# Whole-chunk weight loads outside the expert loops, with the order of the expert rows and gates changed on GpSimd and VectorE

## What is computed

```python
for l in range(DEPTH):                      # DEPTH = 2, D = 1024
    mod = silu_c @ w_ada[l] + b_ada[l]      # [6 * D]: shifts, scales, gains; the same for the context
    h = rmsnorm(x, norm1_g[l]) * (1.0 + sc1) + sh1
    x = x + g1 * token_mixers(h, ...)       # projections, two attentions, a Fourier mix, gated merge, output
    h = rmsnorm(x, norm2_g[l]) * (1.0 + sc2) + sh2
    x = x + g2 * grouped_moe(h, ...)
return rmsnorm(x_lat, final_norm_g)

def grouped_moe(h, ...):
    scores = sigmoid(h @ router_w)          # 16 experts in 4 groups
    # one group for each token, its best 2 of 4 experts, their scores normalized: gate
    hid = silu(h @ w_g[e]) * (h @ w_u[e]) * gate
    return hid @ w_d[e]                     # summed over the experts e of the token
```

## Time and profile before

| | us |
|---|---|
| median of the runs (3 runs, 1233.89 to 1234.39) | 1234.01 |
| the profiled execution, its own time | 1235.45 |
| its span in the profile | 1233.7 |
| PE busy in it | 1182.4 |
| ACT busy | 610.9 |
| DVE busy | 760.0 |
| POOL busy | 58.9 |

### The profile page before, as it was taken

How to read it: one execution, slowest core, us unless ns; L and a number is a source line. 1 busy time by engine, 2 the same in 40 slices (tenths; PEclk the granted TensorE clock), 3 DMA queues, 4 the chain that set the end, 5 groups by cost and what they waited for, 6 DMA issues and landing times.

```text
span 1233.7 us, 17788 instructions
## 1 busy us (share of the span) xinstructions
PE 1182.4 (96%) x6618; PEld 940.8 (76%) x6618; DVE 760.0 (62%) x1237; ACT 610.9 (50%) x962; POOL 58.9 (5%) x77
## 2 busy tenths in 40 slices
PE   6999999899999999999999998999999989999997
PEld 4677555588888878878888886886599987878886
DVE  4563646524423546757985585847746567568995
ACT  4342555633233334446864474536645445457883
POOL 0010000002000000400000010100000001100000
PEclk8999999999999999999999998999989999999999
DMA  9722499738332005767997697332655505759992
GB/s 363 280 88 65 157 392 341 272 103 168 107 103 88 33 1 184 255 219 219 404 351 220 195 337 265 103 103 69 219 183 183 186 18 203 262 186 332 403 378 96
DMA packets 69588, 250.71 MB, mean 203 GB/s; under 512 B 7968, under 2 KB 9152, under 8 KB 69248
## 3 DMA queue, kind: packets, MB, share of 16 engines
q1 hardware_dynamic: 62864, 225.66, 53.3%
q0 software_dynamic: 6640, 23.92, 5.2%
HBM read 237.45 MB, written 12.10 MB: 202 GB/s over the span
## 4 chain that ended last, share of the span: by engine, by line
PE 84%; DVE 5%; DMA 5%; ACT 3%; issue 2%; POOL 1%; SPq 1%; DVEq 0%; ACTq 0%; PEldq 0%; POOLq 0%
PE bank L1798 22%; PE bank L1799 22%; PE bank L1800 22%; DMA raw<-weights 3%; PE bank L1886 3%; PE bank L2066 3%; PE bank L2109 2%; PE bank L2091 2%; DVE lo L1086 1%; PE bank L2001 1%; DMA hu<-by_slot 1%; ACT w_hi L671 1%; PE bank L2350 1%; DMA by_slot<-xtok,slot_i 1%; PE bank L2380 1%
## 5 line engine op out<-in xcount | busy, mean ns | idle before, releaser
L1086 DVE TENSOR_TENSOR lo<-raw,w_hi 128x1024 fp32r<-128x1024 f32 x328 | 401.7, 1234 | 264.1 <-ACT w_hi L671 262.6
L671 ACT CAST w_hi<-raw 128x1024 fp32r<-128x1024 f32 x328 | 343.2, 1051 | 309.8 <-PE bank L1800 298.2
L1798 PE MATMUL bank<-h_hi,w_hi 128*128 128x512 f32 (+1 forms) x512 | 178.3, 348 | 3.1 <-DVE lo L1086 1.5
L1799 PE MATMUL bank<-h_lo,w_hi 128*128 128x512 f32 (+1 forms) x512 | 176.7, 345 | 0.0
L1800 PE MATMUL bank<-h_hi,lo 128*128 128x512 f32 (+1 forms) x512 | 176.3, 344 | 0.0
L1798 PE MATMUL bank<-w_hi,h_hi 128*128 128x512 f32 (+1 forms) x320 | 127.2, 397 | 2.1 <-DVE h_lo L1550 1.4
L1800 PE MATMUL bank<-w_hi,h_lo 128*128 128x512 f32 (+1 forms) x320 | 123.7, 387 | 0.0
L1799 PE MATMUL bank<-lo,h_hi 128*128 128x512 f32 (+1 forms) x320 | 123.6, 386 | 0.0
L1798 PEld LDWEIGHTS bank<-h_hi,w_hi 128*128 128x128 f32 x512 | 97.9, 191 | 21.1 <-issue 6.3
L1800 PEld LDWEIGHTS bank<-h_hi,lo 128*128 128x128 f32 x512 | 97.9, 191 | 11.6
L1799 PEld LDWEIGHTS bank<-h_lo,w_hi 128*128 128x128 f32 x512 | 98.0, 191 | 11.2
(11 more groups left out here) (312 smaller groups left out, 1891.3 us busy)
## 6 DMA issues: line engine op xcount, KB each, us to landing
raw<-weights SPq DMA_DIRECT2D x424, 512.0 KB, 5.9
y_by_slot<-yring POOLq DMA_DIRECT2D x10, 512.0 KB, 7.9
by_slot<-zeros POOLq DMA_DIRECT2D x5, 512.0 KB, 5.6
x<-tokens SPq DMA_DIRECT2D x4, 512.0 KB, 5.7
nab<-na_bias POOLq DMA_DIRECT2D x2, 1024.0 KB, 8.3
hu<-by_slot POOLq DMA_DIRECT2D x2, 1024.0 KB, 11.9
hu<-by_slot POOLq DMA_DIRECT2D x1, 1536.0 KB, 10.2
rp<-rope POOLq DMA_DIRECT2D x2, 512.0 KB, 4.2
```

What stands on the lines that cost most here:

```text
L671: nc.scalar.copy(w_hi[:, g % N_HI, :], raw[:, ring_slot[c], o:o + HALF]).then_inc(hi_done, 1)
L1086: nc.vector.tensor_tensor(lo[:, ring_slot[c], o:o + HALF], raw[:, ring_slot[c], o:o + HALF], w_hi[:, g % N_HI, :].bitcast(F32), ALU.subtra ...
L1798: nc.tensor.matmul(o, l_hi, r_hi, start=start, stop=False)
L1799: nc.tensor.matmul(o, l_hi, r_lo, start=False, stop=False)
```

## The change

Five things are edited.

1. Outside the expert loops a chunk is one load of 1 MB with rows of 8 KB for each partition. `in_halves(p)` says which chunks stay in halves: the 108 of the expert loops. The other 104 are one load each, so that the 424 weight loads become 320. `raw_wait(p, a)` waits for the whole chunk where it comes whole.
2. A whole chunk waits until both halves of the chunk before it in its place have been used.
3. POOL scatters the rows first and then the gates.
4. DVE makes all `xtok` rows in one piece and then the halves of weights that stood between them.
5. PE's wait for a conditioning chunk is one wait in place of two. (`raw_of` and `lo_of` only name what was written out.)

```diff
+        def in_halves(p):
+            kind, n = stream[p]
+            return kind == "mix" and any(first["moe", l] <= n < first["moe", l] + 3 * plan[l]["n_step"] for l in range(DEPTH))
+
         def raw_wait(p, a):
-            return raw_full[ring_slot[p]][a], 16 * (ring_turn[p] + 1)
+            a = a if in_halves(p) else 0
+            return raw_full[ring_slot[p]][a], 16 * sum(ring_slot[b] == ring_slot[p] and (a == 0 or in_halves(b)) for b in range(p + 1))
...
             def load(p, src):
-                for a in range(2):
+                parts_ = ((0, HALF), (HALF, CH)) if in_halves(p) else ((0, CH),)
+                for a, (o, o1) in enumerate(parts_):
                     if ring_prev[p] is not None:
                         kind, n = stream[ring_prev[p]]
                         if kind == "ada":
                             sp.wait_ge(ada_used, n + 1)
                         else:
-                            sp.wait_ge(w_used, 2 * n + a + 1)
-                    o = a * HALF
-                    sp.dma_start(raw[:, ring_slot[p], o:o + HALF], src[:, o:o + HALF]).then_inc(raw_full[ring_slot[p]][a], 16)
+                            sp.wait_ge(w_used, 2 * n + (a + 1 if in_halves(p) else 2))
+                    sp.dma_start(raw_of(p)[:, o:o1], src[:, o:o1]).then_inc(raw_full[ring_slot[p]][a], 16)
...
                 pool.wait_ge(slot_i_done, l + 1)
+                for t in range(nt):
+                    pool.wait_ge(hrows_done, t0 + t + 1)
+                    pool.indirect_dma_start(by_slot, ..., xtok[:, t, :], None).then_inc(hrows_put, 16)
                 pool.wait_ge(g4_done, l + 1)
                 for t in range(nt):
                     pool.indirect_dma_start(gates_by_slot, ..., g4[:, t, :], None).then_inc(gates_put, 16)
-                for t in range(nt):
-                    pool.wait_ge(hrows_done, t0 + t + 1)
-                    pool.indirect_dma_start(by_slot, ..., xtok[:, t, :], None).then_inc(hrows_put, 16)
                 pool.wait_ge(gates_put, 16 * (t0 + nt))
...
-                token_rows(0)
+                for t in range(nt):
+                    # the instruction of token_rows(t)
...
                     for a in (1, 2):
-                        if i == 0 and a < nt:
-                            token_rows(a)
                         more(hs[a])
...
-                    if i == 0 and nt > 3:
-                        token_rows(3)
...
                 pe.wait_ge(*raw_wait(p, 0))
-                pe.wait_ge(*raw_wait(p, 1))
```

More of the change, by code:

```diff
@@ L454, in build, with raw_of, lo_of @@
             last_in[slot_] = p
+        def in_halves(p):
+            kind, n = stream[p]
+            return kind == "mix" and any(first["moe", l] <= n < first["moe", l] + 3 * plan[l]["n_step"] for l in range(DEPTH))
         def raw_wait(p, a):
-            return raw_full[ring_slot[p]][a], 16 * (ring_turn[p] + 1)
+            a = a if in_halves(p) else 0
+            return raw_full[ring_slot[p]][a], 16 * sum(ring_slot[b] == ring_slot[p] and (a == 0 or in_halves(b)) for b in range(p + 1))
+        def raw_of(p):
+            return raw[:, ring_slot[p], :]
+        def lo_of(p):
+            return lo[:, ring_slot[p], :]
         def acc_from(n):
@@ L629, in _ @@
                 pool.wait_ge(slot_i_done, l + 1)
+                for t in range(nt):
+                    pool.wait_ge(hrows_done, t0 + t + 1)
+                    pool.indirect_dma_start(by_slot, bass.IndirectOffsetOnAxis(slot_i[:, t:t + 1], 0), xtok[:, t, :], None)\
+                        .then_inc(hrows_put, 16)
                 pool.wait_ge(g4_done, l + 1)
@@ L670, in half_high @@
                     act.wait_ge(w_used, g - N_HI + 1)
-                nc.scalar.copy(w_hi[:, g % N_HI, :], raw[:, ring_slot[c], o:o + HALF]).then_inc(hi_done, 1)
+                nc.scalar.copy(w_hi[:, g % N_HI, :], raw_of(c)[:, o:o + HALF]).then_inc(hi_done, 1)
             def high(s):
@@ L1085, in half_low @@
                 dve.wait_ge(hi_done, g + 1)
-                nc.vector.tensor_tensor(lo[:, ring_slot[c], o:o + HALF], raw[:, ring_slot[c], o:o + HALF],
+                nc.vector.tensor_tensor(lo_of(c)[:, o:o + HALF], raw_of(c)[:, o:o + HALF],
                                         w_hi[:, g % N_HI, :].bitcast(F32), ALU.subtract).then_inc(lo_done, 1)
@@ L1659, in _ @@
                     dve.wait_ge(shift_in, 32)
-                def token_rows(t):
+                for t in range(nt):
                     (stt(xtok[:, t, :], xtok[:, t, :], rs[:, t:t + 1], shrow[:, t // 2, :], ALU.mult, ALU.add) if ns == 2 else
-                     nc.vector.tensor_scalar(xtok[:, t, :], xtok[:, t, :], rs[:, t:t + 1], None, ALU.mult)).then_inc(hrows_done, 1)
-                token_rows(0)
+                     nc.vector.tensor_scalar(xtok[:, t, :], xtok[:, t, :], rs[:, t:t + 1], None, ALU.mult))                        .then_inc(hrows_done, 1)
                 i0 = 0 if l == 0 else plan[0]["n_step"]
@@ L1845, in wide @@
                 o = kb * width + col
-                return w_hi[:, (2 * s + o // HALF) % N_HI, o % HALF:o % HALF + n], lo[:, ring_slot[at_mix[s]], o:o + n]
+                return w_hi[:, (2 * s + o // HALF) % N_HI, o % HALF:o % HALF + n], lo_of(at_mix[s])[:, o:o + n]
             def feature_half(s, a, results_, nt):
```

2 lines of the change are left out of this document (removed).

## The result

The changed kernel takes 1241.04 us in the median (1236.46 to 1249.19); the kernel before takes 1234.09 us beside it (1231.08 to 1237.91). The ratio is 1.0048, with a 95% interval of 1.0029 to 1.0068: slower by 6 us by the ratio and by 7 in the medians, where 1230.5 us and a gain were forecast.

A forecast was written before the change was run, and what follows sets the result against it. PE, with 84% of the chain, was taken as the bound, so only its waits and the slow clock behind them could change: -3.0 - 0.8 + 0.3 = -3.5 us on 1234.01 gave 1230.5 us, 8-in-10 range 1226.5 to 1235.5.

The forecast's parts named there:

- Place 1: Start, PE's 2.56 us wait for conditioning chunk 7: whole loads land it sooner, 3.0 us gained (bounds 0 to 3.8).
- Rival 1: Long rows bring SP's queue no share, so nothing is gained at the start: 1234.3 us, chance 20%.
- Rival 4: Larger loads also raise the DMA rate, saving 1.1 us more near the start: 1229.4 us, chance 7%.
- Place 2: First layer's expert loop, PE's 2.98 us wait for `hu`: issued at about 518.2, not 519.04, 0.8 us gained.
- I take 1.9 for these: First layer's expert loop: 1.9 us for each of four POOL issues beside DVE, 0.97 for those behind.
- The slow bound: First layer's expert loop: first four issues 2.55 us each, landing 6.3, so `hu` at 521.5, 2.5 us later.
- Rival 3: First layer's expert loop: all eight issues take 2.55 us, gates behind rows make `hu` 7.1 us later: 1238.4 us, 8%.
- DVE's side free: First layer's expert loop: the three `lo` behind the rows end at 507.5 as before, PE's uses come later; no cost.
- The landing of `hu`: Expert loop: time from issue of `hu` until its data is in; no change from before was forecast.
- Place 3: End of the first layer's expert loop, PE's 4.26 us wait for `hdT_lo`: whole loads lose 0.3 us.

The follow-up runs named there:

- The gaps: The whole change plus a one-column DVE copy ahead of the second and third `lo`: 1236.9 us against 1235.27 for the kernel before, ratio 1.0000.
- `hu` ahead: The whole change with `hu`'s first load issued ahead of the wait for the gates: 1232.82 us against 1235.27 for the kernel before, ratio 0.9985.

## Why the prediction was wrong

- **The sign** was wrong by one place of three. Place 1 was right in mechanism, and by the trace its size was at its upper bound: -3.8 us for the chunk itself, not -3.0 (the times, 1.5 to 6.2 us, allow both). The step that undersized it is the landing: chunk 7 was put at 43.2, 0.8 us late, and was there by the end of chunk 6. The sum took POOL's 144 turns at the sizes of packets seen before, and a rate of 397 GB/s; the profile has 426 GB/s from 39 to 43.
- **Rival 1**, that long rows bring SP nothing, is refuted by the 8.0 KB to a packet. The rule of the Trainium skill ("DMA: Bandwidth & Descriptors") that stood behind it, packets of preferably up to 4096 B, doesn't hold for SP's queue here. **Rival 4**, a higher rate, was right in its direction: 383 GB/s from 4 to 12 us and 426 behind it, against 358 and 413, and the chunk that PE waited for at 23.4 came at 22.9. All whole loads gained 5.8 us and chunk 7 alone 3.8 by the ratios, on different chips and within their intervals, so that no run shows what this rival is worth. The two rows are the stretches of the changed kernel (PE busy and operations, granted clock, DMA share, GB/s):

```profile
4.00:12.00 8.00, 3.87 (x8) 1.00 1.00 383
12.00:24.00 12.00, 9.40 (x83) 0.86 1.01 426
```

- **Place 2 failed in the step "I take 1.9 for these", the price of POOL's issues beside DVE.** The issues of the earlier trace rows were read as a spread from 0.96 to 2.55. They are no spread. Each of the slow ones (over 2 us) met a `lo`, and ended 0.83 to 0.84 us behind its end. Here are the rows of the kernel before that the reading left out, POOL's next to the 2.55 us issue at 499.97 of the earlier trace rows, and DVE's `lo` between the rows of tokens of the earlier trace rows:

```profile
502.82 2.02 POOL L632 DMA_INDIRECT gates_by_slot<-g,slot_i  x1 [0.30 <-issue]
505.15 2.03 POOL L636 DMA_INDIRECT by_slot<-xtok,slot_i  x1 [0.30 <-issue]
```

```profile
500.46 1.22 DVE L1086 TENSOR_TENSOR lo<-raw,w_hi 128x1024 fp32r<-128x1024 f32 x1
...
502.79 1.22 DVE L1086 TENSOR_TENSOR lo<-raw,w_hi 128x1024 fp32r<-128x1024 f32 x1
...
505.12 1.22 DVE L1086 TENSOR_TENSOR lo<-raw,w_hi 128x1024 fp32r<-128x1024 f32 x1
```

The issues ended at 502.52, 504.84 and 507.18, the `lo` at 501.68, 504.01 and 506.34. With that rule and three `lo` in a row the second issue is held to 0.9 behind 507.5, 508.4, and everything behind it follows in steps of 1.3. The six left end at 516.2, the gates land 4.5 later as they did, and `hu` goes at about 521.6. The trace has 522.56 on the scale of before, the prediction said 518.2. In numbers of its own: first issue 0.8 us later than forecast, the eight issues 15.75 us from start to end and not 12.8, the gates' landing 4.5 and not 3.7 behind them.
- **The sum of place 2 has a slip besides.** It says that four issues fall beside DVE, and gives 1.9 us to three (500.6, 502.8, 505.0); the fourth, at 507.2, is followed by the next at 508.6. With four, `hu` would go at 519.0, and the 0.8 us gained would be nothing. The slow bound has the same slip: with four issues of 2.55 us it is 523.0 and not 521.5, and the 522.56 of the trace lies inside it. So the place would not have been forecast as a gain, and the range would have reached further up.
- **The rule has an exception in the same trace.** POOL's first issue, at 497.15, began beside the first of two `lo` in a row and ended at 498.35, 0.2 us before the second did:

```profile
496.21 2.35 DVE L1086 TENSOR_TENSOR lo<-raw,w_hi 128x1024 fp32r<-128x1024 f32 x2
```

The same holds in every profile with the gates first. The later issues that met two or three `lo` in a row were held to the last: 2.63 us already in the second layer of the kernel before. Why the first got through was not found.
- **Rival 3** named the right outcome, gates behind rows that make `hu` late, with 1238.4 us and 8%. It expected eight slow issues; there was one very slow one. Its point of decision, `hu` more than 2.7 us later than 519.04, was right: it was 3.5 later.
- The Trainium skill ("SBUF — State Buffer", on who interferes with whom) was weighed and given too little. By it such a DVE operation and a GpSimd one that reads SBUF shut each other out for the whole instruction. The traces agree for `lo` in that a held issue ends 0.83 to 0.92 us behind the end of one. They differ in two points: the hold can last through three instructions in a row (5.45 us), not through one, and beside the run of `xtok`, which has two SBUF inputs too, issues mostly passed in 1.2 to 2.1 us, and in two profiles did not.
- **"DVE's side free"** was right for DVE, and the wrong question. One piece did not delay a `lo` that PE waited for; it removed the rows of tokens between the `lo`, where POOL's issues had been getting through.
- **The landing of `hu`** was taken as 10.2. It was 12.0 here, and 9.6 to 13.6 in the profiles of the twelve runs: this term alone is worth from 0.6 us less to 3.4 us more, and the range had no room for it.
- **The second layer** was given no term, since PE needed `hu` 2.5 us after it landed. The first scatter of rows now took 4.19 us and the second 1.00 (1.55 and 2.63 before). The held issue and the wait for the gates behind it used the 2.5 us up, and 1.98 us more in one profile (3.7 with the clock behind it), 0.3 in another.
- **Place 3**: +0.3 was forecast with bounds of -0.4 and +1.1. ACT's waits changed as described, and the idle time of PE was 4.21 in place of 4.26. No run shows a cost.

Added up in the medians: the whole loads -5.7, the gates' wait and the one piece about +3 each, about 0 in sum, where +6 was measured. The gaps (-4.3) and `hu` ahead (-8.4), taken out of the whole change, point the same way, that the causes are worth more in company, though `hu` ahead is not the order of before, and its 8.4 us are more than the wait for the gates. One reason can be seen in one of the two profiles of the change: together they eat the margin of the second layer, whose wait brings the clock down as well. A longer time at the low clock in the first layer is none: what PE lost there to the clock does not grow with its wait for `hu`. It was 1.7 us behind a wait of 7.0 (rows ahead of gates alone), 1.8 behind 9.5 (the change, second profile), 2.8 behind 8.2 and 3.0 behind 3.2 (chunk 7 whole). So the size of the loss stays open in part; the intervals of these ratios are up to 0.28% wide to either side.

## What to carry to other kernels

Look in the trace at where a slow GpSimd issue ends, not only at how long it takes: if the ends sit at a fixed distance behind one kind of VectorE operation, a row of these can hold the issue until the last of them. Operations that are "free" on VectorE are not free to move when they are what separates the others. When one queue waits for A and then for B, put the transfer that the bottleneck needs behind its own wait alone. And if two queues share the DMA engines, the one with the longer rows gets the larger part: lengthen the rows of the load that is waited for.

## What the runs showed of the hardware

- An indirect-DMA issue on GpSimd takes 0.96 us alone. If it meets a `lo` of VectorE (a subtraction, two inputs in SBUF, 128 x 1024), it mostly ends 0.83 to 0.92 us behind the end of the run of these: of one (up to 2.55 us, and 3.19 where it began under `xtok`), of two (2.63, and 4.31 where it began under `xtok`) or of three (4.18 to 5.45, and 7.05 where it began under more of the `xtok` ahead of them). An operation of 0.16 us that VectorE waits out between two `lo` lets it in. With the gates first, the first issue got through behind the first of two `lo` in a row (1.20 us).
- Beside a run of four `xtok` the first issue, begun at the same place of the program, took 1.25 us in three profiles of kernels with rows first and in one piece, and 7.04 and 7.05 in two others. What decides this was not found.
- Packets of two DMA queues take turns one by one, up to 8 KB each: 109 to 106 with 8 KB against 8 KB, 207 to 200 with 4 KB against 4 KB, and 152 to 151 with 4 KB against 8 KB, whatever bytes they carry.
- The clock does not always fall behind the same idle time. Stretches at the same places of the program, before (205:210, 475:480 and what follows each) and after the change (the same work 4.3 to 6 us sooner), with PE busy and operations, granted clock, DMA share and GB/s:

```profile
205.00:210.00 5.00, 3.62 (x46) 1.00 0.88 323
210.00:215.00 5.00, 4.62 (x52) 1.00 0.82 305
475.00:480.00 5.00, 4.04 (x15) 0.80 0.00 0
480.00:485.00 5.00, 5.00 (x26) 0.86 0.78 256
```

```profile
200.00:205.00 5.00, 3.24 (x40) 0.98 0.88 324
205.00:210.00 5.00, 5.00 (x38) 0.68 0.42 175
470.00:475.00 5.00, 3.54 (x17) 1.00 0.00 0
475.00:480.00 5.00, 5.00 (x28) 1.00 0.60 194
```

Both kernels wait 1.04 us there, for `rows` and then for `rt`. The kernel before kept its clock at the first and lost it at the second, the changed one the other way round. So a drop behind a wait of about a microsecond differs from one execution to the next. Every wait for `hu` of 4.1 us or more lost the clock in these profiles. Of the shorter ones those of 1.98, 2.92, 2.98 and 3.21 us lost it too, and one of 3.18 and one of 1.44 us did not. How much of the spread of the times comes from this was not measured.
